# Squares summed by fp32r passes, and VectorE's work laid out anew, in a two-block kernel

## What is computed

```python
def gated_deltanet(h, w_in, conv_w, a_log, dt_bias, norm_w, w_out):
    proj = h @ w_in
    qkv, z, b, a = jnp.split(proj, ...)
    qkv = jax.nn.silu(causal_depthwise_conv(qkv, conv_w))
    q, k, v = jnp.split(qkv, [GDN_DQK, 2 * GDN_DQK], axis=-1)
    q = jnp.repeat(l2norm(q...) * HEAD_DIM ** -0.5, rep, axis=2)
    k = jnp.repeat(l2norm(k...), rep, axis=2)
    ...
    o = gated_delta_rule(q, k, v, g, beta)
    o = o * lax.rsqrt(jnp.mean(o * o, -1, keepdims=True) + NORM_EPS)
    o = (o.astype(h.dtype) * norm_w) * jax.nn.silu(z)
    return o.reshape(B, S, GDN_DV) @ w_out
```

## Time and profile before

| | us |
|---|---|
| median of 3 runs | 2680.88 |
| lowest and highest | 2679.38 to 2681.06 |
| profiled execution, own time | 2680.55 |
| its span, first to last instruction | 2678.9 |
| PE busy in it | 2628.5 (98%) |
| DVE, ACT, POOL busy | 1997.6, 1221.8, 865.7 |

### The profile page before, as it was taken

How to read it: one execution, slowest core, us unless ns; L and a number is a source line. 1 busy time by engine, 2 the same in 40 slices (tenths; PEclk the granted TensorE clock), 3 DMA queues, 4 the chain that set the end, 5 groups by cost and what they waited for, 6 DMA issues and landing times.

```text
span 2678.9 us, 44567 instructions
## 1 busy us (share of the span) xinstructions
PE 2628.5 (98%) x16843; PEld 2205.9 (82%) x16843; DVE 1997.6 (75%) x2523; ACT 1221.8 (46%) x1604; POOL 865.7 (32%) x646
## 2 busy tenths in 40 slices
PE   6999999999999999999999999999999999999998
PEld 4798899899887888888888888899777778888887
DVE  1487887788798687777777777689999996655554
ACT  2365556545665445343343343354333334444344
POOL 1076777777767404500000000014555550000000
PEclk8999999999999999999999999999999999999999
DMA  9966776776676776666666666655555555666664
GB/s 364 361 222 216 232 244 217 233 236 220 211 250 202 229 202 221 190 193 189 189 192 191 188 190 193 189 160 174 169 170 168 173 176 180 191 189 187 190 204 153
DMA packets 283972, 552.47 MB, mean 206 GB/s; under 512 B 16881, under 2 KB 54322, under 8 KB 282674
## 3 DMA queue, kind: packets, MB, share of 16 engines
q1 hardware_dynamic: 263488, 473.49, 57.2%
q0 software_dynamic: 19472, 76.06, 8.0%
q10 hardware_dynamic: 866, 0.80, 0.1%
HBM read 548.19 MB, written 2.10 MB: 205 GB/s over the span
## 4 chain that ended last, share of the span: by engine, by line
PE 82%; DVE 14%; DMA 2%; issue 1%; SPq 1%; ACT 0%; DVEq 0%
PE pg L1201 40%; PE pd L1201 18%; PE pg L930 5%; PE pg L943 4%; PE pg L1188 4%; DVE pd L2068 3%; DVE arena L2068 2%; PE pg L962 2%; DVE arena L2142 1%; DMA wr<-in_gdn_w_in 1%; PE pd L856 1%; DVE arena L2302 1%; DVE arena L2234 1%; DVE arena L2237 1%; DVE arena L2208 1%
## 5 line engine op out<-in xcount | busy, mean ns | idle before, releaser
L1794 ACT ACTIVATE wh<-wr 128x1024 fp32r<-128x1024 f32 x616 | 652.9, 1061 | 927.0 <-PE pg L1201 581.4
L2341 DVE TENSOR_TENSOR wl<-wr,wh 128x1024 fp32r<-128x1024 f32 x615 | 771.5, 1266 | 381.4 <-ACT wh L1794 378.1
L670 POOL TENSOR_TENSOR wl<-wr,wh 128x1024 fp32r<-128x1024 f32 x195 | 485.3, 2497 | 266.3 <-ACT wh L1575 127.3
L1201 PE MATMUL pg<-wh,hh 128*128 128x512 f32 x1344 | 528.9, 394 | 0.3 <-DVE hl L2417 0.3
L1201 PE MATMUL pg<-wl,hh 128*128 128x512 f32 x1344 | 527.3, 392 | 0.0
L1201 PE MATMUL pg<-wh,hl 128*128 128x512 f32 x1344 | 525.7, 391 | 0.0
L1575 ACT ACTIVATE wh<-wr 128x1024 fp32r<-128x1024 f32 x216 | 227.8, 1057 | 324.9 <-PE pg L943 163.5
L1201 PEld LDWEIGHTS pg<-wh,hh 128*128 128x128 f32 x1344 | 252.5, 188 | 59.5 <-DVE wl L2341 2.4
L943 PE MATMUL pg<-hh,wh 128*128 128x256 f32 x1024 | 299.9, 293 | 0.8 <-ACT arena L1635 0.8
L1201 PEld LDWEIGHTS pg<-wh,hl 128*128 128x128 f32 x1344 | 252.4, 188 | 56.4
L1201 PEld LDWEIGHTS pg<-wl,hh 128*128 128x128 f32 x1344 | 252.3, 188 | 54.4
(11 more groups left out here) (451 smaller groups left out, 4873.1 us busy)
## 6 DMA issues: line engine op xcount, KB each, us to landing
wr<-in_w_in SPq DMA_DIRECT2D x224, 512.0 KB, 3.8
wr<-in_ffn_w_gu SPq DMA_DIRECT2D x176, 512.0 KB, 3.8
wr<-in_gdn_w_in SPq DMA_DIRECT2D x128, 512.0 KB, 4.4
arena<-in_mod_w POOLq DMA_DIRECT2D x60, 1024.0 KB, 6.6
wr<-in_ffn_w_down SPq DMA_DIRECT2D x88, 512.0 KB, 4.6
arena<-in_mod_w SPq DMA_DIRECT2D x32, 1024.0 KB, 13.6
wr<-in_gdn_w_in SPq DMA_DIRECT2D x128, 256.0 KB, 3.2
wr<-in_gdn_w_out SPq DMA_DIRECT2D x56, 512.0 KB, 4.7
```

The costliest lines, as they stand in the source:

```text
L670: nc.gpsimd.tensor_tensor(wl[c % RING][:], wraw[c % 4], wh[c % RING][:].bitcast(F32), ALU.subtract)\
L1201: m = nc.tensor.matmul(halves(bank)[:, h, :], act[x][:, k0 + k, h * P:(h + 1) * P], w[s][:, k, :], skip_group_check=True, start=(first and ...
L1794: a(wh[c % 4][:], wraw[c % 4], ACT.Copy).then_inc(s_hc, 1)
L2341: v.tensor_tensor(wl[c % 4][:], wraw[c % 4], wh[c % 4][:].bitcast(F32), ALU.subtract).then_inc(s_lc, 1)
```

## The change

- **Sums of squares.** DVE writes the squares over `vtok`, ACT squares q and k once more and writes them rounded to fp32r over `Xb` (`sqh`), GpSimd subtracts and writes the rest over `vtok` (`sql`, fp32r); PE multiplies each by ones, 4 fp32r matmuls in place of 2 float32 ones, and waits for GpSimd. On GpSimd the subtraction stands behind the first chunk of the next group and the load 0 that follows it.
- **Gate projection.** ACT copies its first part ahead of rounding chunk 1, which stood ahead of it.
- **DVE.** `squares` moves ahead of `o1`; the output copy `o0` gets a slot of its own, so that the loop has 19 slots in place of 18; the halves and transposes are put in other slots; a half fewer sums in PSUM. In the last group the low parts of the output move.

```diff
-MOD_HALVES = {0: (0, 1), **{t: (t - 1,) for t in range(3, 11)}, 11: (10, 11), 14: (12,), 15: (13,), 16: (14, 15)}
-V_TURNS = {3: (0, 2), 4: (2, 4), 8: (4, 6), 9: (6, 8), 10: (8, 10), 12: (10, 14), 13: (14, 16)}
-LATE_LOWS = (0, 1, 2, 4, 6)
+MOD_HALVES = {0: (0, 1), **{t: (t - 1,) for t in range(3, 12)}, 14: (11,), 15: (12,), 16: (13,), 17: (14, 15)}
+V_TURNS = {3: (0, 2), 9: (2, 4), 10: (4, 6), 11: (6, 8), 12: (8, 14), 13: (14, 16)}
+LATE_LOWS = (0, 1, 2, 5, 15)
...
+            def squares_low(g):
+
+                pool.wait_ge(s_sq1, g + 1)
+                pool.wait_ge(s_sqh, g + 1)
+                nc.gpsimd.tensor_tensor(sq_s[1][:], fl(vtok), sq_s[0][:].bitcast(F32), ALU.subtract).then_inc(s_sql, 1)
...
                         low(it + 2, t)
                         if t < 2:
                             mod_load(it * 8 + 40, t)
+                        if t == 0:
+                            squares_low(it + 1)
...
-                pe.wait_ge(s_sq1, it + 1)
+                pe.wait_ge(s_sql, it + 1)
...
                 for n in range(2):
-                    m = nc.tensor.matmul(pd[0][:, n * 512:(n + 1) * 512], ones[:], sqb[:, n * 512:(n + 1) * 512],
-                                         start=True, stop=True)
+                    for i in range(2):
+                        m = nc.tensor.matmul(pd[0][:, n * 512:(n + 1) * 512], ones_r, sq_s[i][:, n * 512:(n + 1) * 512],
+                                             start=(i == 0), stop=(i == 1))
...
+            def squares_high(g):
+
+                act.wait_ge(s_qk, g + 1)
+                a(sq_s[0][:], fl(qk), ACT.Square).then_inc(s_sqh, 1)
...
                     silu_qk(it + 1)
+                    squares_high(it + 1)
                     silu_v(it + 1)
...
-                yield
                 if more:
                     z_out(it + 1, 0)
+                yield
...
-                v.tensor_tensor(sqb, fq, fq, ALU.mult).then_inc(s_sq1, 1)
+                v.tensor_tensor(fl(vtok), fl(qk), fl(qk), ALU.mult).then_inc(s_sq1, 1)
...
                 mod_sum(it, 0)
+                yield
                 PEw("o0")
...
                 yield
-                if not mods:
+                if mods:
+                    squares(it + 1)
+                else:
                     low(0, 0, 0)
                 PEw("o1")
...
-                if mods:
-                    squares(it + 1)
...
-                    held = range(4, 16) if 2 <= half < 8 else range(8) if 8 <= half < 12 else range(0)
+                    held = range(4, 16) if 2 <= half < 8 else range(6) if 8 <= half < 11 else range(0)
...
-                    if isinstance(j, int) and t == 16:
+                    if isinstance(j, int) and t == 17:
                         o_low(0)
                         o_low(1)
```

More of the change, by code:

```diff
@@ L221, in build @@
         zt = take(8, P)
+        xb_at = at[0]
         Xb = take(8, P)
@@ L229, in build @@
                   for i in range(2))
-        sqb = Xb.rearrange("p a b -> p (a b)")
         db_at = at[0]
@@ L271, in build @@
         ones_r = ones[:].bitcast(F32R)
+        sq_s = [over("sqh", arena_at + 4 * xb_at, 8 * P), over("sql", arena_at + 4 * vtok_at, 8 * P)]
         rowm = over("rowm", arena_at + 4 * rowm_at, VH, P)
@@ L429, in build @@
         s_sq1 = sem("s_sq1")
+        s_sqh = sem("s_sqh")
+        s_sql = sem("s_sql")
         s_ot = sem("s_ot")
@@ L728, in _ @@
                 low(1, t)
+                if t == 1:
+                    squares_low(0)
             pool.wait_ge(s_md, 32)
@@ L1753, in _ @@
             gh(1, 1)
+            squares_high(0)
             z_out(0, 0)
@@ L2153, in squares @@
                 dve.wait_ge(s_qk, it + 1)
-                fq = qk.rearrange("p a b -> p (a b)")
-                v.tensor_tensor(sqb, fq, fq, ALU.mult).then_inc(s_sq1, 1)
+                v.tensor_tensor(fl(vtok), fl(qk), fl(qk), ALU.mult).then_inc(s_sq1, 1)
             v.memset(Ub[64:P, :, 0:64], 0.0)
@@ L2315, in iteration @@
                 steps = delta(j, True)
-                for t in range(18):
+                for t in range(19):
                     next(steps, None)
@@ L2366, in _ @@
                     mod_half(LATE, n // 2, n % 2, range(2, 12) if 1 <= n < 6 else range(0))
-                if t == 16:
+                if t == 17:
                     for i in range(3):
```

## The result

| | before | after |
|---|---|---|
| median, us | 2680.63 (2679.38 to 2681.06, 4 runs) | 2718.12 (2715.20 to 2718.64, 4 runs) |
| profiled execution, us | 2680.55, span 2678.9 | 2717.90, span 2716.3 |
| one group of heads, us | 92.33 | 97.03 to 98.38 |

The changed kernel is slower: its time is 1.0138 times that before, 95% interval 1.0121 to 1.0156. The forecast was 2716.9 us.

What follows compares the result with a forecast made beforehand. PE, busy 98% of the span, was taken as the bound. Terms 27.3 + 10.2 + 5.4 + 0.5 - 3.6 - 3.5 = 36.3 us on 2680.55 gave 2716.9 us, 1.3% slower; range 2698 to 2732 us.

Steps and rivals of the forecast that it cites:

- Half 11 and load 7: In seven groups GpSimd's load 7 waits for the moved half 11; chunk 19's low part is late, PE idle 3.90 us each: 27.3 us.
- The clock: Behind PE's idle 3.90 us the granted clock halves, in six of seven groups, costing 1.7 us each: 10.2 us.
- The sums of squares: PE does 0.80 us less per group, but ACT's extra operation makes `on` late by as much: nothing gained.
- GpSimd's subtraction: GpSimd's added operation contends with DVE's `on` (0.7 us) and halves 0 and 1 (0.2 us), six times: 5.4 us lost.
- The levels: Moving two transpose pairs ahead of the level-16 product removes PE's 0.59 us wait there, six times: 3.6 us gained.
- The last group: Moving `o_low` from slot 4 takes back 3.5 us of idle time and half clock; longer waits at its start cost 0.5.
- One working among the rivals: Rival, GpSimd isn't held: chunk 19 on time if load 7 is under 3.1 us late; 2669 to 2673 us, chance 0.07.
- The other forecasts for the profile of the changed kernel: Signs expected: GpSimd waits some 8 us ahead of load 7, half clock behind most stalls, no idle time at level 16.
- the idle time of 1 to 1.5 us behind the sums: Sign expected: after sums of squares of 0.92 us per group, PE idles about 1 to 1.5 us for `on`.
- GpSimd catches up with one stall: After chunk 19, low parts follow at 2.42 us each, PE's products take 2.76 us per chunk, so no further stall.
- the clock that holds: Rival: the clock mostly doesn't cost, as idle time is split or it falls while nothing runs; 2706.7 us, chance 0.16.
- The 1.77 us that I took for a small disturbance: Half 12's time before the change, used as the disturbed length of half 11 in the stall's upper bound, 4.3 us.

## Why the prediction was right, step by step

**Half 11 and load 7** (27.3 us forecast): 27.4 us. The mechanism, the place, the count and the size hold: seven waits, GpSimd held by half 11 ahead of load 7. The half took 1.54 us, the load came after 0.64, the subtraction 0.80 later. The 3.90 us of the forecast run from the time at which chunk 19 would have started, so the measured value must be taken in the same way. Before, chunk 19 started 0.35 us after the first of four transposes:

```profile
501.91 0.60 PE L856 MATMUL pd<-ident,arena 128*128 128x128 f32 x4
```

The same transposes start at 614.83 in the changed kernel, so chunk 19 could have started at 615.18 and was 3.81 us late. The bracket's 3.56 is smaller since it starts at 615.43, where the last transpose left the array. With this 0.25 us added to each of the seven waits, 25.7 becomes 27.4 us.

**The clock** (10.2 us forecast): 16.0 us. Three stretches of 3.41 us and four of 6.83 make 37.6 us at half clock, in which PE stood idle for 5.5; in the other 32.1 us it did half of what it does at full clock, so 16.0 us are lost. The difference of two kernels agrees: the changed kernel lies 39.6 us above the one with half 11 wholly back; 27.4 of them are the waits at chunk 19, and the second kernel has 3.5 us of waits at level 32 that the first lacks, so 39.6 - 27.4 + 3.5 = 15.7 us are left for the clock. Two parts of the step were too small: it fell in seven groups, not six, and stayed down for 6.8 us, not 3.4, in four of them.

**The sums of squares** (0 forecast): right, and for the reason given. ACT's last step ahead of `on` started 431.60 - 429.56 = 2.04 us after the start of the next group's first chunk before, and starts 644.54 - 641.40 = 3.14 us after it now, so the extra squares made it 1.10 us later. The transposes come 4.59 us after that chunk's start before and 4.68 us now: the 0.80 us are gone. What the forecast missed is where PE spends them: only 0.13 us ahead of the transposes, and 0.66 us earlier, at the gate's copy (643.50 - 642.72 from start to start, less the 0.12 between such matmuls). By these times an earlier copy would only move the wait to `on`; no run tried it.

**GpSimd's subtraction** (5.4 us forecast): nothing of it shows, and this step failed. `on` took 1.24 us, where the earlier trace rows had 1.31, because GpSimd's operation of that moment (642.10 + 2.85 = 644.95) ended 0.17 us after `on` began at 644.78; the waits of PE at the first level, on whose way halves 0 and 1 stand, are 2.8 us in total in both kernels. Without the wait and the clock a group takes 97.03 - 3.81 - 1.7 = 91.5 us, against 92.33 before, so the change loses nothing else in it.

**The levels** (3.6 us forecast): right, and a little small, for these groups are 0.8 us shorter than before, of which 0.7 is the wait at level 16 from start to start. It holds as long as half 11 isn't ahead of level 32. In the changed kernel level 32 has no wait, because half 11 left its slot; the versions with half 11 back and the transposes as changed show the wait that these would have made there.

**The last group** (3.5 less 0.5 us forecast): only 0.7 us. From its first product to the end of the span the kernel before takes 2678.9 - 798.27 = 1880.6 us and the changed one 2716.3 - 836.34 = 1880.0. The 2.21 us are gone, but smaller waits came (1.07 us for `ol`, 0.35 at a level), and the half clock is still there: it now follows the waits at the start of the group, which are longer than before. The version with the old low parts is only 1.0 us slower than the one with the new, which agrees with a small net gain.

**The total** came within 1.2 us partly by luck, because errors cancel: the clock was 5.8 us too low and the gain of the last group 2.3 too high, the term for GpSimd's subtraction 5.4 too high and the gain at the levels some 2 too low. The main term was not luck. One working among the rivals is wrong and changed nothing in the sum: load 7 could come up to 499.04 - 494.33 = 4.7 us late before chunk 19 waits, not 3.1. The other forecasts for the profile of the changed kernel held (a wait of some 8 us on GpSimd ahead of load 7; the wait at level 16 gone), except the idle time of 1 to 1.5 us behind the sums, which is 0.13.

**One sentence of the forecast was half right:** "GpSimd catches up with one stall". For PE it does. For DVE the catching up is itself the trouble, and this is why three ways of taking the stall away (half 11 back in SBUF, load 7 later, half 11 in slot 13) recovered only 6 to 18 of the 39.6 us. Of the rivals, the clock that holds would have given 2706.7 us; in the changed kernel it fell in seven groups of seven. The two waits of 1.88 us with a clock that held, beside four with one that fell, show that it isn't certain to fall after a wait of that length.

**What stays open.** Why the idle time left after the clock's fall sorts the stretches of 3.4 and 6.8 us cleanly in the changed kernel and not in all others. Why single waits at level 32 are three or four times as long as the usual 0.45 us. Whether half 11 in slot 14 with its sum in PSUM would have saved a part: place and memory were put back together, or the place alone. Of the 21.6 us between the kernels with half 11 in slot 13 and in slot 11 with PSUM, the named waits make up about 17 by the brackets; there are some 20 more of them in the first, and the 0.25 us that a bracket lacks would make up the rest. This is an estimate.

## What to carry to other kernels

When an operation moves on one engine, look for a queue of another engine in which something waits for it and count what stands behind that wait; then count a second time, for the burst in which the held engine catches up, since the burst can stop whoever works on SBUF beside it. Undo such a change wholly before judging its parts: half 11 in its old place without its old memory was worth 8 us of 40, with it all of them. Compare a forecast lateness with starts of instructions, not with the idle time in a bracket. And a wait taken from one level of a chain that is near its limit comes back at the next; look whether the group's length changed, not whether the wait is gone.

## What the runs showed of the hardware

- **Two engines at SBUF.** The same two steps of DVE over 512 columns, with both large inputs in SBUF, took 1.53 and 1.54 us with GpSimd standing still, and 4.20, 7.19, 6.67 and 9.26 us beside its runs. This is no slowing in proportion: in three kernels the two steps ended 1.34 us after GpSimd's run did (506.48 and 507.82; 623.57 and 624.91; 614.26 and 615.60), whatever the length of the run. The first of the two steps is the one that is held; in the changed kernel the second, at 624.15, took 0.75 us again:

```profile
617.72 6.40 DVE L2089 SCALAR_TENSOR_TENSOR arena<-arena,condt 128x512 f32<-128x512 f32 x1
```

It ends at 624.12, 0.55 us after GpSimd's run. The same holds all through the traces of the two kernels and of six experiments (150 to 900 us): of the steps of halves with both large inputs in SBUF, 208 began inside a GpSimd subtraction and took over 0.9 us, and each ended 0.54 to 0.56 us after the end of that subtraction, or of the last one of its run, if subtractions followed less than 0.08 us apart. Only three more began inside one, in its last 0.35 us or less, and they took 0.90 us at most. A pause of 0.26 us was enough to let one step through: with load 7 later, the first step of half 12 ended 0.55 us after the run of three, and the second was held until 0.55 us after the fourth subtraction. So DVE waits for a pause of GpSimd. Steps with a PSUM operand beside such a run kept to 0.75 to 0.78 us each. The trace of before had it too, had I set the end of half 12 beside GpSimd's row there:

```profile
498.79 2.41 POOL L670 TENSOR_TENSOR wl<-wr,wh 128x1024 fp32r<-128x1024 f32 x1 [1.24 <-ACT wh L1575]
```

It ends at 501.20 and half 12, started at 500.76, at 502.53: 1.33 us later. The 1.77 us that I took for a small disturbance was the same wait with little of GpSimd's operation left (0.44 us). The page "GPSIMD Engine Reference" of the Trainium skill ("Key points") names contention of GpSimd with DVE instructions that have two SBUF inputs; the runs agree; the size, up to 9.26 us in place of 1.53, is theirs, and so is the reading that the whole run has to end first.
- **The clock.** After idle time of 3.56 us (the changed kernel; 4.36 in one group), 3.1 us (2.57 in one) and 3.3 us (4.34 in one; two of the experiments), the granted clock fell to 0.50 (1.2 in place of 2.4 GHz) in seven groups of seven each time. After 2.69 us it fell once, and after 1.88 us in four groups of six. After 1.45, 1.68 and 0.66 us (half 11 in slot 13) it didn't fall. The time at half clock was 3.4 us or twice that.
- **A wait in GpSimd's queue.** From the end of the half on DVE to the record of the load that waits for it: 0.64 us; the load's own record is 0.77 us, and the next subtraction starts 0.80 us after it. So in this kernel the subtraction behind a held load starts no sooner than 1.44 us after the half that holds it.
